# Early expert rows multiplied in another stage, and bf16 parts of gate weights made ahead: a two-layer transformer kernel

## The reference

```python
q = (xc @ peer_wq).reshape(TOKEN_CHUNK, PEER_HEADS, PEER_DQ)
...                                   # top 16 of 128 keys twice, top 16 of the 256 sums
e = jnp.take_along_axis(cand_i, pos, axis=-1)
g = jax.nn.softmax(top_s, axis=-1).astype(xc.dtype)
u = peer_u[e]
h = jax.nn.gelu(jnp.einsum('cd,chkd->chk', xc, u))
return jnp.einsum('chk,chkd->cd', g * h, peer_v[e])
```

## Time and profile before

| | |
|---|---|
| median of 3 runs | 3294.23 us (3291.33 to 3294.79) |
| profiled execution | 3291.42 us, span 3289.6 us |
| granted TensorE clock, mean | 0.914 |
| PE busy | 2826.8 us (86%) |
| DVE busy | 2313.7 us (70%) |
| ACT busy | 1257.3 us (38%) |
| POOL busy | 813.3 us (25%) |

### The profile page before, as it was taken

One profiled execution on the slowest core, in us unless ns is written; L12 is line 12 of the kernel. 1 busy time (PEld: TensorE's weight loads), 2 busy tenths in 40 slices (PEclk: granted clock), 3 DMA queues, 4 the chain that ended last, 5 costly groups with the idle time before them and its releaser, 6 DMA issues. The chain is left out here.

```text
span 3289.6 us, 57570 instructions
## 1 busy us (share of the span) xinstructions
PE 2826.8 (86%) x22507; PEld 1834.6 (56%) x22507; DVE 2313.7 (70%) x4080; ACT 1257.3 (38%) x2060; POOL 813.3 (25%) x475
## 2 busy tenths in 40 slices
PE   6896989976899999999699999577787768779987
PEld 3453455545577777777446566356565544334466
DVE  4794377889788888888672677578888843567732
ACT  3232124348333333333312576444454423133221
POOL 0650045530445455555202221100000011000000
PEclk9658999987999999999899999689899978889998
DMA  3001245555999999999333320411111015143140
GB/s 126 1 1 58 103 133 170 172 180 233 360 377 361 362 362 364 362 362 350 126 94 106 88 59 20 136 32 32 32 42 32 20 56 195 58 128 102 51 141 33
DMA packets 278230, 495.00 MB, mean 150 GB/s; under 512 B 18784, under 2 KB 177120, under 8 KB 275872
## 3 DMA queue, kind: packets, MB, share of 16 engines
q1 hardware_dynamic: 241184, 358.24, 32.0%
q0 software_dynamic: 36864, 134.23, 10.4%
HBM read 435.21 MB, written 57.21 MB: 150 GB/s over the span
## 5 line engine op out<-in xcount | busy, mean ns | idle before, releaser
L1347 PE MATMUL banks<-gated_hi,v_hi 128*128 128x384 bf16 (+2 forms) x1536 | 335.0, 273 | 0.5 <-DVE gated_lo L1318 0.5
L1347 PE MATMUL banks<-gated_lo,v_hi 128*128 128x384 bf16 (+2 forms) x1536 | 335.0, 273 | 0.0
L1347 PE MATMUL banks<-gated_hi,v_lo 128*128 128x384 bf16 (+2 forms) x1536 | 335.0, 273 | 0.0
L1185 POOL DMA_INDIRECT gathered_u<-in_u_rows,first_tile_rows x128 | 212.5, 1660 | 288.4 <-DVE gathered_dots L1293 156.5
L815 POOL TENSOR_TENSOR early_u_lo<-early_u_raw,early_u_hi 128x1024 bf16<-128x1024 f32 x64 | 156.0, 2439 | 336.2 <-ACT early_u_hi L875 336.2
L1190 POOL DMA_INDIRECT gathered_v<-in_v,first_tile_rows x128 | 175.3, 1369 | 201.7 <-DVE x_tokens L1285 181.8
L1792 POOL TENSOR_TENSOR gates_w_lo<-gates_raw,gates_w_hi 128x1024 bf16<-128x1024 f32 x24 | 53.4, 2227 | 600.1 <-ACT gates_w_hi L2083 600.1
L1347 PEld LDWEIGHTS banks<-gated_hi,v_hi 128*128 128x128 bf16 x1536 | 150.3, 98 | 56.4 <-issue 1.0
L846 PE MATMUL banks<-act_hi,early_u_hi 128*128 128x384 bf16 x512 | 168.0, 328 | 12.2 <-POOL early_u_lo L815 11.7
L1334 PE MATMUL banks<-act_hi,u_hi 128*128 128x384 bf16 x512 | 168.1, 328 | 11.6 <-DVE u_lo L1271 11.6
L1285 DVE SCALAR_TENSOR_TENSOR x_tokens<-gathered_v,gathered_weights,x_tokens 128x1024 f32<-128x1024 f32 x128 | 164.1, 1282 | 6.1 <-DVE gathered_weights L1276 1.6
(11 more groups left out here) (597 smaller groups left out, 7910.9 us busy)
## 6 DMA issues: line engine op xcount, KB each, us to landing
v_raw<-in_v SPq DMA_DIRECT2D x128, 512.0 KB
early_u_raw<-in_u SPq DMA_DIRECT2D x64, 512.0 KB, 3.9
u_raw<-in_u SPq DMA_DIRECT2D x64, 512.0 KB
gate_tables<-gate_piece SPq DMA_DIRECT2D x12, 2048.0 KB, 6.3
gate_group<-gate_tables SPq DMA_DIRECT2D x32, 768.0 KB
ffn_up_raw<-in_ffn_up SPq DMA_DIRECT2D x20, 1024.0 KB, 7.5
early_gelu<-early_gelu_columns SPq DMA_DIRECT2D x64, 192.0 KB, 1.9
gelu_early_rows<-early_gelu SPq DMA_DIRECT2D x32, 384.0 KB
```

The source lines that it names most:

```text
L1185: pool.indirect_dma_start(gu[:, n % GROUP, :], None, u_table, bass.IndirectOffsetOnAxis(ap=rows.index[:, 0, n:n + 1], axis=0)).then_inc(gu ...
L1347: m = pe.matmul(ps[:, bank, to:to + width], v[:, j, cols], w[:, j, tok:tok + width], start=start and n == 0 and to == 0, stop=stop and n = ...
```

## The change

1. 16 of the 64 early groups of u move from `pick_experts` (now 12 per tile) to `spread_gates`, 16 passes after each of the 24 batches. Their low parts are made by VectorE there (the first three still by GpSimd). uh and ul get three buffers. The spreading uses six PSUM banks, its loops are written out, and u tiles for `run_experts` are loaded at its end.
2. The keys and four rows of u are loaded by the projection's SyncE list.
3. High and low parts of the 16 gate pieces are made beside the projection by ScalarE and GpSimd and stored to DRAM; `rwkv_heads` loads them as they are. The 8 branch pieces are cast and subtracted as before, with two raw buffers, each loaded later than before.
4. Semaphores are cleared once more, before the second norm.

```diff
+EARLY_PICKING = 48
+EARLY_RING = 3
...
         with nc.Block() as block:
+            if split is not None:
+                @block.gpsimd
+                def _(pool):
+                    for p in range(split.count):
+                        split.low(pool, p)
...
+                if split is not None:
+                    for p in range(split.RAW):
+                        split.load(sp, p)
                 each(sp, load, 2)
                 if along is not None:
                     along(sp)
+                if split is not None:
+                    for p in range(split.count):
+                        split.store(sp, p)
+                        if p + split.RAW < split.count:
+                            split.load(sp, p + split.RAW)
+                    split.finish(sp)
...
                     act.copy(wh[:, slot, :, 0:r.width], raw[:, slot, :, 0:r.width]).then_inc(hi_done, 1)
+                    if split is not None:
+                        for p in split.beside_chunk(c):
+                            split.high(act, p)
...
+    def bank(self, i):
+        return 4 + i % 4 if i < EARLY_PICKING else 6 + i % 2
...
-        PER_TILE = EARLY // NT
+        PER_TILE = EARLY_PICKING // NT
...
+    RING = 6
+    NBATCH = DT // NB
+    PASSES = (EARLY - EARLY_PICKING) * 3 * KD // NBATCH
+
+    def finished(i):
+
+        return [EARLY_PICKING + n for n in range(EARLY - EARLY_PICKING)
+                if PASSES * i < 3 * KD * (n + 1) <= PASSES * (i + 1)]
...
                 sp.dma_start(iota[:], k.dram["iota"]).then_inc(loaded, 16)
-                for j in range(LIVE):
-                    rows.load_u(k, sp, 0, 0, j)
                 for j in range(GROUP):
                     rows.load_v(k, sp, j, j)
                 rows.load_gelu(k, sp, 0, 0)
...
+                for i in range(NBATCH):
+                    for n in finished(i):
+                        early.store(sp, n)
+                        early.load(sp, n + 4)
+                    if (i + 1) % (TCH // NB) == 0:
+                        store((i + 1) // (TCH // NB) - 1)
+                sp.wait_ge(early.u_lo, EARLY)
+                for j in range(LIVE):
+                    rows.load_u(k, sp, 0, 0, j)
...
+                for i in range(NBATCH):
+                    batch(i, i % 2, i // 2)
+                    for n in finished(i - 2) if i >= 2 else []:
+                        if n + EARLY_RING < EARLY:
+                            early.low(dve, n + EARLY_RING)
...
+                for i in range(NBATCH):
+                    for n in range(4):
+                        quad(4 * i + n)
+                    early.dense(pe, PASSES)
...
+                for i in range(NBATCH):
+                    for n in range(4):
+                        keep(4 * i + n)
+                    for n in finished(i):
+                        early.gelu(act, n)
+                        early.high(act, n + EARLY_RING)
...
+class GateParts:
+
+    RAW = 3
...
+    def beside_chunk(self, c):
+
+        return {1: range(0, 2), 2: range(2, 8), 3: range(8, self.count)}.get(c, ())
+
+    def load(self, sp, p):
+        if p >= self.RAW:
+            sp.wait_ge(self.w_low, p - self.RAW + 1)
+        c, half = divmod(p, 2)
+        first = RW_COLS + NSA_COLS + half * D + c * P
+        sp.dma_start(self.raw[:, p % self.RAW], self.w_in[:, :, first:first + P]).then_inc(self.landed[p % self.RAW], 16)
+
+    def high(self, act, p):
+        act.wait_ge(self.landed[p % self.RAW], 16 * (p // self.RAW + 1))
+        if p >= 2:
+            act.wait_ge(self.stored[p % 2], 16 * (p // 2))
+        act.copy(self.parts[:, p % 2, 0], self.raw[:, p % self.RAW]).then_inc(self.w_high, 1)
+
+    def low(self, pool, p):
+        pool.wait_ge(self.w_high, p + 1)
+        pool.tensor_tensor(self.parts[:, p % 2, 1], self.raw[:, p % self.RAW], self.parts[:, p % 2, 0],
+                           ALU.subtract).then_inc(self.w_low, 1)
+
+    def store(self, sp, p):
+        sp.wait_ge(self.w_low, p + 1)
+        sp.dma_start(self.k.dram["gate_parts"][p], self.parts[:, p % 2]).then_inc(self.stored[p % 2], 16)
...
+    k.clear_semaphores()
     experts = ExitStack()
...
                 def load_gate(p):
                     if p >= 3:
-                        sp.wait_ge(w_low, p - 2)
...
+                        sp.wait_ge(multiplied, p - 2)
+                    sp.dma_start(parts[:, p % 3], k.dram["gate_parts"][p]).then_inc(w_landed[p % 3], 16)
+
+                def load_branch(q):
+                    if q >= 2:
+                        sp.wait_ge(w_low, q - 1)
+                    sp.dma_start(raw[:, q % 2], w_nsa[:, :, q * P:(q + 1) * P]).then_inc(branch_landed[q % 2], 16)
...
                 for p in range(2 * KD, 3 * KD):
                     store_gate(p)
-                    if p + 4 < 3 * KD:
-                        load_gate(p + 4)
+                    if p + 3 < 3 * KD:
+                        load_branch(p + 3 - 2 * KD)
...
-                for p in range(3 * KD):
-                    pool.wait_ge(w_high, p + 1)
-                    pool.tensor_tensor(wl[:, p % 2], raw[:, p % 3], wh[:, p % 2], ALU.subtract).then_inc(w_low, 1)
+                for q in range(KD):
+                    pool.wait_ge(w_high, q + 1)
+                    pool.tensor_tensor(parts[:, (2 * KD + q) % 3, 1], raw[:, q % 2], parts[:, (2 * KD + q) % 3, 0], ALU.subtract).then_inc(w_low, 1)
...
                             gate_out(p)
-                            if p + 2 < 3 * KD:
-                                gate_high(p + 2)
+                            if p + 3 < 3 * KD:
+                                branch_high(p + 3 - 2 * KD)
...
-                        gate_high(2 * KD + 1)
+                        branch_high(2)
...
-                        if invert and s == 1 and i >= 1:
-                            gate_high(2 * i + 1)
-                        if invert and s == 4:
-                            gate_high(2 * i + 2)
+                        if invert and i == KD - 1 and s in (1, 4):
+                            branch_high(s // 4)
```

More of the change, by code:

```diff
@@ L741, in pick_experts @@
+def pick_experts(k, pq, sel, rows, early):
     nc, ps = k.nc, k.ps
@@ L790, in _ @@
             def _(sp):
[L791 to L807, removed]
+                for i in range(EARLY_PICKING):
+                    early.store(sp, i)
+                    early.load(sp, i + 4)
             @block.gpsimd
             def _(pool):
[L811 to L815, removed]
+                for i in range(EARLY_PICKING + EARLY_RING):
+                    early.low(pool, i)
             @block.tensor
             def _(pe):
-                pe.wait_ge(loaded, 32)
+                pe.wait_ge(early.keys_landed, 32)
                 def score(t):
@@ L838, in turn @@
                     last.then_inc(turned, 1)
[L840 to L848, removed]
                 score(0)
@@ L851, in _ @@
                     for n in range(PER_TILE):
-                        column(PER_TILE * t + n)
+                        early.dense(pe, 3 * KD)
                         if n == 3 and t + 1 < NT:
@@ L867, in keep @@
                     last.then_inc(kept, 1)
[L869 to L881, removed]
+                for i in range(EARLY_RING):
+                    early.high(act, i)
                 keep(0)
-                u_high(0)
-                u_high(1)
                 for t in range(NT):
                     for n in range(PER_TILE):
-                        gelu(PER_TILE * t + n)
-                        u_high(PER_TILE * t + n + 2)
+                        early.gelu(act, PER_TILE * t + n)
+                        early.high(act, PER_TILE * t + n + EARLY_RING)
                         if n == 3 and t + 1 < NT:
@@ L901, in _ @@
             def _(dve):
-                dve.wait_ge(loaded, 32)
+                dve.wait_ge(early.keys_landed, 32)
                 def best_of(n, values, rest, best_v, best_i, turn):
@@ L999, in load_gelu, with spread_gates @@
                      ).then_inc(self.ge_landed[slot], 16)
-def spread_gates(k, sel, rows):
+def spread_gates(k, sel, rows, early):
     nc, ps = k.nc, k.ps
@@ L1087, in _, with quad @@
-                four_banks(0)
-                with pe.Fori(1, DT // 32) as i:
-                    four_banks(i)
+                def quad(q):
+                    if q >= RING:
+                        pe.wait_ge(kept, q - RING + 1)
+                    i = q // 4
+                    if q % 4 == 0:
+                        pe.wait_ge(first_hot, i + 1)
+                        pe.wait_ge(gates_on, 2 * i + 2)
+                    for n in range(4):
+                        slot, tok = i % 2, 4 * (q % 4) + n
+                        g, t = tok // TI, tok % TI
+                        pe.matmul(ps[:, q % RING, n * P:(n + 1) * P], first[:, slot, g, :, t], g_hi[:, slot, g, :, t],
+                                  start=True, stop=False)
```

(7 more changed lines are left out.)

198 lines of the change are left out of this document (121 added, 77 removed).

## The result

| | kernel before | changed kernel |
|---|---|---|
| median of the runs | 3294.23 us | 3238.9 us (3236.99 to 3240.04) |
| ratio, 95% interval | | 0.9833 [0.9816, 0.985] |
| profiled execution | 3291.42, span 3289.6 | 3238.18, span 3236.4 |

Faster by 55.3 us. The forecast was 3250, in 3240 to 3270: the sign and the mechanism held, the time lies 1.1 us under the range. Measured beside other runs of the kernel before, the changed kernel had 3235.75 against 3292.44, ratio 0.9831.

A forecast was written before the change was run, and what follows sets the result against it. Bounds: TensorE in projection and picking, VectorE in spreading, a ring of waits between three engines in the heads. +1.2 -2.2 -43.2 +15.6 +2.0 +1.0 +2.5 -17.0 -3.8 = -43.9 gives 3247.5 profiled, 3250 us as median; range 3240 to 3270.

The forecast's parts named there:

- Picking: Expert picking with 16 fewer columns: VectorE becomes the bound, exponent wait goes, 279.4 us become 236.2, so -43.2.
- the same reading of the other tiles ... Sum 233.3 us: Picking: VectorE's work in the four tiles, read from the trace before, taken as 233.3 us in all.
- Spreading: Gate spreading with 16 more columns: VectorE stays the bound, 13 subtractions of 1.2 us each add +15.6.
- The term for the low clock: Spreading: TensorE at half clock for the first 10 to 20 us costs +2.0.
- (b): Spreading: TensorE's clock keeps alternating at 0.75, 142 us instead of 125, +17, total 3267; chance 0.10.
- (d): Spreading: TensorE stays at its lower clock level throughout, 213 us against 125, +88, total 3338; chance 0.04.
- The last eight take 4 x 6.8 = 27 us from 388, the last store is down at about 416: Projection: the last gate-piece splits finish before TensorE's end at 420.4, cost 0, with 4 us of margin.
- rival (a): Projection runs over: split pairs take 8.5 us instead of 6.8, last store at 430, +12, total 3262; chance 0.12.
- Heads: Heads: removed GpSimd subtractions no longer delay VectorE's copies, -17.0 in the turns and -3.8 before turn 0; casts worth nothing.
- longer than the excess, so all counts: -17.0 (bounds 0 and -19): Heads: TensorE's waits exceed the excess of thirteen VectorE predicated copies, so the whole excess is gained, -17.0.
- (c): Heads don't give: removed delays turn up again, since the ring waits for ScalarE or loads; +17 to +21, 3270; chance 0.10.
- (e): Heads' last turn: branch loads come late, 5 x 1 to 6 us, total 3265; chance 0.05.

The follow-up runs named there:

- heads_no_gpsimd: Kernel before, with the heads' GpSimd subtractions of gate pieces 2 to 15 writing one column instead of 128x1024; 3261.58 us, ratio 0.9894.
- branch_three: Changed kernel with a third buffer for the branch's raw weights, each load issued one piece earlier; 3233.32 us, ratio 0.9822.

## Why the prediction was right or wrong

**Picking: right, under-sized by 4.4.** No wait for the exponent, VectorE the bound, tiles of 57 to 58 us. The step "the same reading of the other tiles ... Sum 233.3 us" carried the kernel before's own stalls along: it read the multiplications of 4.09 us as their natural length, and concluded that GpSimd was the one held. They are 2.29 alone. All eight of those multiplications were stalled before, seven of the changed kernel's sixteen products are (12.7 us of excess by the groups, 14.4 before): 1.7 of the 4.4. Some 1.1 more is a shorter tail behind the last tile; the other 1.6 is spread over small differences, not settled.

**Spreading: right, over-sized by 3.2.** VectorE's 13 subtractions took 1229 ns each, 16.0 with 15.6 forecast, but each starts 1.14 us behind the one before it (785.09 and 786.23 for two one-hots of 1.24), so they made the stage 14.8 longer. The term for the low clock, +2.0, was not due: VectorE stayed the bound from the first batch (busy 11.86 us from 668 to 680), although TensorE's clock was 0.64 there. The end, from the start of the last one-hot to the experts' first cast, took +3.1 (12.5 to 15.6 us) with 3.5 forecast. Rivals (b) and (d) fell with a clock of 0.97.

**Earlier loads and the projection: a gain of 0.6 for 2.2; the step that failed here is "The last eight take 4 x 6.8 = 27 us from 388, the last store is down at about 416".** The cast of the eighth from the end started at 391.7, behind the last chunk's, and the last store was issued at 423.3 and down at 425.9, 34 us later. Lines of GpSimd and VectorE show the first loss:

```profile
392.82 5.42 POOL L1548 TENSOR_TENSOR gate_parts<-v_raw,gate_parts 128x1024 bf16<-128x1024 f32 x1 [2.32 <-ACT gate_parts L1544]
...
391.83 4.42 DVE L356 TENSOR_TENSOR peer_wq_w_lo<-peer_wq_raw,peer_wq_w_hi 128x4096 bf16<-128x4096 f32 x1 [9.24 <-ACT peer_wq_w_hi L314]
```

GpSimd, second to start, stood 3.3 us until VectorE's subtraction was over. Then two stores (issued at 400.4 and 404.6) took 6.8 and 5.4 us to land, where 3 were forecast, and ScalarE stood for both. The five pieces behind them came at 3.2 us each, no slower than the forecast's pairs. The rest of rival (a) did not come: VectorE's subtractions kept 4.43 us, GpSimd's took 5.42 twice of 16 times, and ScalarE's last chunk cast moved from 379.04 to 388.20, 6.1 of it beyond the stage's own shift of 3.1, where 8 to 9 were forecast: hidden.

**Clearing: right** (1.1 measured, 1.2 forecast). The other 2.3 us of the first row are within the 2.9 us by which code that is the same in both varied, so no run shows them to be the change's.

**Heads: right in mechanism, under-sized by 7.7, and this is the step that put the time under the range.** The copies named as stalled are short now, 13 of 15, and the casts are worth nothing, as argued. The step that failed is "longer than the excess, so all counts: -17.0 (bounds 0 and -19)": it took the VectorE excess as an upper limit. heads_no_gpsimd shows 4.2 us per turn for 2.45 of excess; of the missing 10.7 us in the six turns, 8.8 are TensorE's longer busy time, at the lower clock level. In the changed kernel turns 1 to 6 are 26.8 us shorter (4.5 each), with 15.8 of the forecast's 20.8 for them; up to turn 1 it is 3.4 with 5.0 forecast, and the last full turn and the end are 1.7 longer. Rivals (c) and (e) fell. The change's heads give slightly less than heads_no_gpsimd's (28.5 against 30.9 in the profiles), more than all of it in the last full turn and the end (143.2 us for 136.7). TensorE is busy 100.8 us there for 94.6, with the same products, at a clock of 0.83 for 0.86. branch_three shows that it isn't the late loads, and why the clock is lower stays open.

**Sum.** The errors are +2.2, +1.6, -4.4, -3.2, -1.1, -7.7, +3.3: -9.3. Without the last, and without the 2.3 us of the first that are not the clearing's, it would be -14.9: neither is shown to be the change's, and both brought the time nearer to the forecast by luck. The heads' term is what carried the time past the range, which took a gain of up to 54 in its own text (-38 to -52 for the forecast, 3240 as its low end) and had no case in which two terms came out better at once.

## What to carry to other kernels

Before a duration from a trace is used as the cost of an instruction, look for the same instruction elsewhere with GpSimd idle: 4.09 read like a natural length and was 2.29 plus a stall. A stall on a ring between three engines can be worth more than its own length (here 1.7 times), and removing what delays the culprit (the casts) only moves it to the next instruction. When work is moved in front of a stage's end, ask what the block waits for last: here it was a store's landing, and one moved wait gave 3.7 us at that place.

## What was not expected of the hardware

- GpSimd is not held for one VectorE instruction only: beside back-to-back two-input instructions of 1.22 us, subtractions of 2.12 us took 14.2, 18.4 and 19.8 (3 of 13).
- A VectorE product of 2.29 us becomes 3.9 to 4.25 when a GpSimd subtraction stands ahead of it, and none of the seventeen profiles has one between 2.3 and 3.8; the reduction beside it keeps 2.29 at all times. Short ones pay too: 0.29 us becomes 1.51.
- Two kernels that differ in nothing before norm2 reach it 2.9 us apart (312.2 and 315.1).
- With the same code there, the stretch from TensorE's first product of the scores to the first pick came at a clock of 0.78 (behind idle times of 2.5 to 3.3 us) or of 1.00 (behind 2.4 to 2.6), and that alone is 1.6 us.
